# Splitting the expert weight loads of a mixture-of-experts encoder between two DMA queues

## The reference

```python
aff = softmax(t @ w_router)                       # per request group
gate, idx = top_k(aff.T, cap)                     # 32 + 64 tokens per expert
def expert(wg, wu, wd, ix, g):                    # 16 experts
    xe = t[ix]                                    # 96 rows of 1024
    he = silu(xe @ wg) * (xe @ wu)                # 1024 -> 2816
    return (he @ wd) * g[:, None]                 # 2816 -> 1024
y = zeros.at[idx].add(ye)                         # added to the residual
```

## Time and profile before

| | us |
|---|---|
| median of 3 runs (2209.09 to 2210.94) | 2210.21 |
| the profiled execution, as timed | 2212.8 |
| its span, first to last instruction | 2211.0 |
| PE busy in it | 2128.8 (96%) |
| DVE busy | 1582.0 (72%) |
| ACT busy | 1370.8 (62%) |
| POOL busy | 238.7 (11%) |
| hardware DMA queue of SP, share of 16 engines | 69.6% |

### The profile page before, as it was taken

One profiled execution on the slowest core, in us unless ns is written; L12 is line 12 of the kernel. 1 busy time (PEld: TensorE's weight loads), 2 busy tenths in 40 slices (PEclk: granted clock), 3 DMA queues, 4 the chain that ended last, 5 costly groups with the idle time before them and its releaser, 6 DMA issues.

```text
span 2211.0 us, 27257 instructions
## 1 busy us (share of the span) xinstructions
PE 2128.8 (96%) x10388; PEld 1592.4 (72%) x10388; DVE 1582.0 (72%) x1249; ACT 1370.8 (62%) x1102; POOL 238.7 (11%) x137
## 2 busy tenths in 40 slices
PE   6999999999968999999999999999999999999997
PEld 5867888887756767777677776767767677777765
DVE  5374363233456888888888888888888888888885
ACT  5364364122225777777777777777777777777764
POOL 2202120000130001010101102011010201101010
PEclk9999999999988999999999999999999999999999
DMA  5111141113436999999999999999999999999995
GB/s 232 58 36 67 58 144 60 64 58 115 162 118 236 373 370 366 376 371 385 364 368 385 367 378 370 373 373 370 378 365 380 365 374 385 367 376 374 375 372 184
DMA packets 71389, 623.97 MB, mean 282 GB/s; under 512 B 8272, under 2 KB 8656, under 8 KB 18608
## 3 DMA queue, kind: packets, MB, share of 16 engines
q1 hardware_dynamic: 63264, 595.62, 69.6%
q0 software_dynamic: 7648, 27.40, 4.4%
q10 hardware_dynamic: 432, 0.34, 0.0%
HBM read 609.70 MB, written 13.63 MB: 282 GB/s over the span
## 4 chain that ended last, share of the span: by engine, by line
PE 82%; DMA 7%; DVE 6%; ACT 4%; issue 1%; POOL 0%; ACTq 0%; SPq 0%; DVEq 0%; POOLq 0%
PE PS L527 25%; PE PS L529 25%; PE PS L528 25%; DMA x_w_raw<-in_w_expert_gate 5%; DVE x_w_low L1160 4%; ACT x_w_high L1090 3%; PE PS L625 2%; PE PS L610 2%; PE PS L872 1%; DMA x_w_raw<-in_w_expert_up 1%; PE PS L638 1%; PE PS L536 1%; PE PS L815 1%; PE PS L736 0%; DMA cst<-in_consts 0%
## 5 line engine op out<-in xcount | busy, mean ns | idle before, releaser
L1160 DVE TENSOR_TENSOR x_w_low<-x_w_raw,x_w_high 128x2048 fp32r<-128x2048 f32 (+1 forms) x382 | 1174.5, 3086 | 241.9 <-ACT x_w_high L1090 239.6
L1090 ACT ACTIVATE x_w_high<-x_w_raw 128x3072 fp32r<-128x3072 f32 (+1 forms) x384 | 980.0, 2558 | 266.2 <-PE PS L529 190.9
L527 PE MATMUL PS<-x_w_high,xT_high 128*96 128x512 f32 (+1 forms) x1536 | 580.5, 378 | 9.7 <-DVE x_w_low L1160 7.6
L529 PE MATMUL PS<-x_w_high,xT_low 128*96 128x512 f32 (+1 forms) x1536 | 575.4, 375 | 0.0
L528 PE MATMUL PS<-x_w_low,xT_high 128*96 128x512 f32 (+1 forms) x1536 | 573.4, 373 | 0.0
L527 PEld LDWEIGHTS PS<-x_w_high,xT_high 128*96 128x96 f32 x1536 | 248.3, 162 | 105.6 <-DVE x_w_low L1160 18.6
L529 PEld LDWEIGHTS PS<-x_w_high,xT_low 128*96 128x96 f32 x1536 | 248.1, 162 | 90.0
L528 PEld LDWEIGHTS PS<-x_w_low,xT_high 128*96 128x96 f32 x1536 | 248.8, 162 | 85.1 <-issue 0.2
L527 PE MATMUL PS<-x_w_high,hidden_high 128*96 128x512 f32 x704 | 281.3, 400 | 0.0
L529 PE MATMUL PS<-x_w_high,hidden_low 128*96 128x512 f32 x704 | 276.7, 393 | 0.0
L528 PE MATMUL PS<-x_w_low,hidden_high 128*96 128x512 f32 x704 | 275.9, 392 | 0.0
(11 more groups left out here) (185 smaller groups left out, 1774.4 us busy)
## 6 DMA issues: line engine op xcount, KB each, us to landing
x_w_raw<-in_w_expert_gate SPq DMA_DIRECT2D x96, 1536.0 KB, 8.4
x_w_raw<-in_w_expert_up SPq DMA_DIRECT2D x96, 1536.0 KB, 8.8
x_w_raw<-in_w_expert_down SPq DMA_DIRECT2D x96, 1536.0 KB, 8.3
x_w_raw<-in_w_expert_gate SPq DMA_DIRECT2D x32, 1024.0 KB, 7.5
x_w_raw<-in_w_expert_up SPq DMA_DIRECT2D x32, 1024.0 KB, 7.4
x_w_raw<-in_w_expert_down SPq DMA_DIRECT2D x32, 1024.0 KB, 7.0
w_raw<-in_w_in SPq DMA_DIRECT2D x20, 1024.0 KB, 4.8
x<-in_x_sample SPq DMA_DIRECT2D x8, 512.0 KB, 13.5
```

The lines of the kernel that those rows point to most:

```text
L527: mm(out, sh, mh, start=first, stop=False)
L529: return mm(out, sl, mh, start=False, stop=last)
L1090: a_(xh[:, w % SPLITS, 0:n], xraw[:, w % RAWS, 0:n], ACT.Copy).then_inc(x_high, 1)
L1160: return v.tensor_tensor(out, src, high.bitcast(F32), ALU.subtract)
```

## The change

SP loads only the units with even numbers. ACT issues the loads of those with odd numbers on its own queue, in its own instruction stream: load 1 ahead of its first high copy, load 3 behind the copy of unit 2, and then in the loop body of each even u, behind the high copy of unit u+3, the load of unit u+5. Each of these loads still waits for the low part of the unit four before it.

```diff
             with sp.Fori(0, E) as e:
-                for w, (kind, q, c) in enumerate(XU):
+                for w in range(0, NXU, 2):
                     sp.wait_ge(x_split, e * NXU + w + 1)
...
+            def load_odd_unit(e, w):
+
+                b = w % RAWS
+                act.wait_ge(x_split, e * NXU + w + 1)
+                act.dma_start(xraw[:, b, 0:unit_width(w)], unit_source(e, w)).then_inc(x_loaded[b], 16)
...
+            stage_done(act, 6)
+            load_odd_unit(0, 1)
             out_done(act, NT - 1, 1)
             unit_high(0, 0)
             for b in range(2):
                 act.wait_ge(S("n2", f"stored{b}"), 48)
             for w in range(1, SPLITS):
                 unit_high(0, w)
+            load_odd_unit(0, 3)
...
                         unit_high(e + 1, w - NXU)
+                    w = u + 5
+                    if u % 2 == 0 and w < NXU:
+                        load_odd_unit(e, w)
+                    elif u % 2 == 0 and not last:
+                        load_odd_unit(e + 1, w - NXU)
                     if u == 0:
```

## The result

The changed kernel took 2410.77 us (median of 4 runs, 2386.14 to 2431.01) against 2210.57 us for the kernel before in the same series (2209.09 to 2211.14): ratio 1.0873, 95% interval 1.0839 to 1.0906. It is slower, as forecast, by 200 us where 218 were forecast (2430). The profiled execution took 2406.81 us, with a span of 2405.0 us, 194.0 more than the span of before. The runs of before agree within 2.1 us, those of after lie up to 45 us apart. The run at 2431.01 counts as slow and stays out of the ratio, which is why that isn't 2410.77 / 2210.57.

The account below looks back on a forecast made before the run. PE was taken as the bound, the DMA engines close behind. The late-load chain was to add 218 us (15.9 experts from 94.8 to 108.5 us), start and end 0, giving about 2430 us, range 2270 to 2600.

Parts of the forecast that it names:

- The chain: Expert stage, odd unit w: copy of w-2 starts, load w issues, lands, copy of w starts; 108.5 us per expert.
- Issue cost: ACT's load instruction, 0.33 us, issues 0.2 us after the copy's start and runs beside it, hidden under 2.77 us of copying.
- Rival 1: ACT's load issue waits for the copy's end, lengthening the loop: about 2620 us; chance 0.12.
- The table load: On ACT between landing and copy of unit 3: adds 1.3 us to the chain per expert.
- Rival 2: PE's clock falls as well because PE idles in the expert stage: 80 us more, about 2510; chance 0.10.
- Rival 3: The queues hardly share, so only units beside gather and scatter are late: 50 us, 2260 in all; chance 0.11.
- Rival 4: Not slower: two queues land odd loads within 7 us and PE's idle goes: 11 us less, about 2199; chance 0.07.
- L: Time of an odd load from issue to landing; large 6.7 us alone, 8.8 by the old stage's medians.
- Size of L: Load-latency bounds: alone no cost, middle 103.6 us per expert, upper with sharing queues 112.3; taken 108.5.
- P: Length of the chain, L + 0.3 us, to fit PE's time for two units; about 9.95 for large pairs, upper bound.
- d: Delay of the even load behind the odd one: about 2.4 us in the old spacing, 9.3 - P in the chain.
- The number of experts: 191 odd loads in the chain, the worth of 15.9 experts, each 108.5 instead of 94.8 us: 218 us.

Follow-up runs that it names:

- ahead: The changed kernel with ACT's load of odd unit w placed ahead of the high copy of unit w-2, not behind it: 2262.61 us, ratio 1.0249 to the kernel before.
- copy_end: The changed kernel with ACT's odd loads also waiting for the end of the high copy ahead of them: 2685.13 us, ratio 1.2156 to the kernel before.
- after_two_products: The changed kernel with the third product of each split matmul left out in the expert stage, a third less PE work: 2412.83 us, one run.
- two_queues: Separate program, only weight loads, alone or in pairs on one or two queues: one large load on each queue landed after 10.0 and 10.2 us.
- small_even: The changed kernel with SyncE loading only an eighth of each even unit's columns (output not the reference's): 2201.75 us, ratio 0.9968 to the kernel before.
- streams: Separate program, only streams of 22 large loads, on one or two queues: 6.3 us a load with one in flight, 4.16 with two, 3.82 with four.

## Why the prediction came out

- **The chain.** Right: copy of w-2, issue, landing, copy of w. ahead takes the place away and 9.3 of 12.2 us go; copy_end lengthens one link and the expert grows with it.
- **Issue cost.** Right: issue 0.2 us after the copy's start and inside it, 0.34 us long. Rival 1 (about 2620) needed an issue at the copy's end. copy_end makes that kernel, at 2685 us. What the prediction quotes beside this, from the Trainium skill's "Advanced Engine Details and Errata", "Sequencer and Instruction Queues", is the other direction: it has engine instructions queued while a control instruction executes, while 1443.0 in the earlier trace rows and 1985.74 above are a control instruction and a DMA going while an engine instruction runs. "The trace agrees" says too much there.
- **The table load.** The sum has 1.3 us for it. Landing to copy of unit 3 did take 1.4 us, but the next load does not wait for it: load 5 goes 0.96 us before the copy of unit 3 starts, during the table load, and not 0.2 us after it. In the chain the table load costs next to nothing, about 0.1 us.
- **Rival 2**, the clock: out as a cost, though the sign named for it, a granted clock under 1 in the expert stage, was there. It fell to 0.97, yet in after_two_products it fell to 0.87 and cost nothing.
- **Rival 3**, queues that hardly share: out by two_queues, where both loads of a pair land after about 10 us.
- **Rival 4**, not slower: the point from which it decides, L below 7.6, was right. small_even has L at 6.7 to 6.9 and is not slower. In the change L was 8.84 for large odd units.
- **Size of L.** This is where the sum was off, in both bounds. The lower one, "alone", can't be had with a neighbour in flight: streams shows 8.0 us for two. The "middle", 103.6 us with medians of the old stage, was therefore nearer to a floor than to a middle. The upper one took a pair of large loads on two queues at 9.95 us for P; measured was 8.84 + 0.3 = 9.1. A part of that is the offset between the two loads. P = 9.95 puts d, by which the even load follows, at 9.3 - 9.95: the even load 0.65 us ahead of the odd one. Measured, the even load followed, by 0.3 to 2.4 us for most units (2.1 in the timeline above) and by 1.1 on the mean of the large odd ones, so the odd load had more of the engines and the even one paid (9.30 on the mean). The prediction's own L = 10.3 - d gives 9.2 for d = 1.1; the last 0.3 us to 8.84 stay open. For small odd units I took 7.3 and measured 7.84. By kind, upper bound and measured: six pairs large with large, with the table load, 61.0 and 56.4 us; three with a small even unit 28.5 and 27.2; three with a small odd one 22.8 and 23.9. 108.5 was a choice between the two bounds, and 107.0 came: 1.5 us x 15.9 = 24 us of the sum. That it came so near is luck of the choice; the range from 103.6 to 112.3 is what had been worked out.
- **The number of experts** in the chain, 15.9, was right: 15.9 x 12.2 = 194, the difference of the spans.
- **Start and end** cost nothing, as worked out: -1.7 us at the first copy.
- **What was to be seen.** PE's idle is 8.8 in 93 us, not 10 or more: its matmuls ran a little slower at 0.97 (the costliest group 387 ns on the mean, 378 before), which makes it busy 60.7 us longer in the stage. ACT's waits moved from PE to landings, an expert takes 107.0 us, in the 103 to 113 that I gave, and the DMA share is 0.83 to 0.93, 0.86 over the stage, in the 85 to 90%. From the second on, single experts lie between 100.7 and 114.8 us (by the copy of their unit 0). Why they and the runs spread so much more than before was not tried.

The rule that the prediction weighed from the Trainium skill's "DMA: Bandwidth & Descriptors", "Queues, rings and completion order", in which each DMA engine takes turns between its queues, agrees with the pair at 10.0 and 10.2 us. The fit in "Anatomy of one DMA" is given there for GpSimd's software path, and the prediction applied it to a hardware queue. Its estimate of 5.6 us for a large load alone is below the 6.2 us measured on an otherwise idle chip and the 6.7 of the kernel.

The kernel before has four raw buffers on one queue, and still its large loads take 8.4 to 8.8 us and not the 14.7 of streams with four in flight. Its trace says why: a load goes every 94.8 / 24 = 3.95 us and takes 8.33 on the mean, so that 2.1 are in flight, not four. What stays open: how the 2.2 us that two early queues cost divide between order and anything else wasn't separated.

## What to carry to other kernels

When a load is moved to an engine that also uses the data, look at what stands ahead of it in that engine's order: a load behind a copy that waits for an earlier load makes a chain whose period is a full latency with that many loads in flight. Take the latency from a stretch with the same number of loads in flight (their mean latency by the distance of their issues), never from a lone one. A second queue brought no rate here (3.82 us a load either way at four in flight), but it gives up the order, so that the load needed first is no longer served first.

## What the runs showed of the hardware that was not expected

- Large loads of 1.5 MB: 6.3 us each one at a time (250 GB/s), 4.16 with two in flight (378 GB/s), 3.82 with four (412 GB/s), on one queue or two.
- Two large loads on two queues end after 10.0 and 10.2 us (six repeats: 9.8 to 10.6), on one queue after 6.1 and 9.4, the second issued 0.4 us behind the first. Counted from the first issue, the first to land comes about 4 us later on two queues, and the last about 0.6 us later too.
- A 1 MB load started beside a 1.5 MB one on the other queue lands after 9.0 us, though it has a third less to bring than the large one, which lands after 8.8.
- The granted clock fell to 0.87 in the expert stage when PE had a third less to do, and the time stayed within 0.1%, though a matmul of the costliest group took 433 ns and not 387: where PE idles, a lower clock was no cost.
- A DMA instruction on ACT can also run beside a table load, and so ahead of the copy that it stands behind: with all loads on ACT, one went at 1508.02 inside a table load of 1.28 us, and the copy started at 1509.05.

```profile
1507.75 1.28 ACT L1091 ACT_TABLE_LOAD   x1 [4.47 <-DMA x_w_raw<-in_w_expert_up]
1508.02 0.34 ACTq L1084 DMA_DIRECT2D x_w_raw<-in_w_expert_up  x1
```
